# Four changes of order in a two-layer encoder kernel: a copy ahead of maxima, two projection blocks ahead of a value product, final transposes behind a loop, filler products around the opening's sums

## The reference

```python
for l in range(DEPTH):
    mod = cond @ ada_w[l] + ada_b[l]
    sh1, sc1, g1, sh2, sc2, g2 = jnp.split(mod, 6, axis=-1)
    h = modulate(rms_norm(x, norm_mix_g[l]), sh1, sc1)
    if l % 2 == 0:
        y = stick_window_mixer(h, ab_w_in[j], ab_sinks[j], ab_w_out[j])
    else:
        y = hgrn2_mixer(h, hg_w_in[j], lb_all[l], hg_onorm_g[j], hg_w_out[j])
    x = x + g1[:, None, :] * y
    h = modulate(rms_norm(x, norm_ffn_g[l]), sh2, sc2)
    x = x + g2[:, None, :] * conv_ffn(h, ...)
return rms_norm(x, final_g)
```

## Time and profile before

| | |
|---|---|
| median of 3 runs | 1359.72 us |
| lowest, highest | 1358.35, 1359.87 us |
| the profiled execution: its own time | 1360.04 us |
| its span | 1358.2 us, 17432 instructions |
| mean granted clock of TensorE | 0.993 of 2.4 GHz |
| busy: PE, DVE, ACT, POOL | 97%, 60%, 41%, 3% of the span |
| the chain that ended last | PE 89%, DVE 5%, ACT 2% |
| DMA | 160.38 MB, mean 118 GB/s |

### The profile page before, as it was taken

How to read it: one execution, slowest core, us unless ns; L and a number is a source line. 1 busy time by engine, 2 the same in 40 slices (tenths; PEclk the granted TensorE clock), 3 DMA queues, 4 the chain that set the end, 5 groups by cost and what they waited for, 6 DMA issues and landing times.

```text
span 1358.2 us, 17432 instructions
## 1 busy us (share of the span) xinstructions
PE 1323.5 (97%) x6281; PEld 1083.0 (80%) x6281; DVE 808.7 (60%) x1197; ACT 558.1 (41%) x837; POOL 46.9 (3%) x92
## 2 busy tenths in 40 slices
PE   6999998899999999999999999999999999999998
PEld 5877776777888888888778888888788888888786
DVE  5745557567666656436697777775765455552423
ACT  6656554334333333212255555553343333332212
POOL 1000000000000000001100000000000000000000
PEclk9999999999999999999999999999999999999998
DMA  9543431153544555465622222224523333332232
GB/s 336 167 124 109 125 109 32 46 164 103 150 142 143 150 146 147 141 184 190 210 82 78 76 65 63 74 67 125 155 78 95 105 93 93 94 107 93 82 100 81
DMA packets 190148, 160.38 MB, mean 118 GB/s; under 512 B 5271, under 2 KB 163176, under 8 KB 190098
## 3 DMA queue, kind: packets, MB, share of 16 engines
q1 hardware_dynamic: 177696, 116.34, 28.5%
q0 software_dynamic: 11856, 42.68, 10.4%
q10 hardware_dynamic: 546, 0.69, 0.1%
HBM read 157.59 MB, written 2.10 MB: 118 GB/s over the span
## 4 chain that ended last, share of the span: by engine, by line
PE 89%; DVE 5%; ACT 2%; SPq 1%; issue 1%; DMA 1%; DVEq 0%; ACTq 0%
PE proj L1603 61%; PE z L1603 22%; PE obank L1603 3%; PE misc L1603 2%; SPq L479 1%; DVE ada_sum L1118 1%; DMA w_raw<-ab_w_in 1%; DVE normed L1056 0%; ACT w_hi L621 0%; DVE hT_lo L1062 0%; SPq L489 0%; DVE soft L1220 0%; ACT q_sb L741 0%; DVE w_lo L1018 0%; DVE xT L1410 0%
## 5 line engine op out<-in xcount | busy, mean ns | idle before, releaser
L1603 PE MATMUL proj<-hT_hi,w_hi 128*128 128x512 f32 x1112 | 441.5, 397 | 4.6 <-DVE hT_lo L1062 4.1
L1603 PE MATMUL proj<-hT_hi,w_lo 128*128 128x512 f32 x1112 | 433.7, 390 | 0.0
L1603 PE MATMUL proj<-hT_lo,w_hi 128*128 128x512 f32 x1112 | 433.4, 390 | 0.0
L1018 DVE TENSOR_TENSOR w_lo<-w_raw,w_hi 128x1024 fp32r<-128x1024 f32 x189 | 231.2, 1224 | 338.6 <-ACT w_hi L621 338.6
L621 ACT ACTIVATE w_hi<-w_raw 128x1024 fp32r<-128x1024 f32 x191 | 202.0, 1059 | 442.7 <-PE proj L1603 261.2
L1603 PEld LDWEIGHTS proj<-hT_hi,w_hi 128*128 128x128 f32 x1112 | 209.2, 188 | 57.2 <-DVE hT_lo L1062 8.0
L1603 PEld LDWEIGHTS proj<-hT_hi,w_lo 128*128 128x128 f32 x1112 | 209.0, 188 | 44.4
L1603 PEld LDWEIGHTS proj<-hT_lo,w_hi 128*128 128x128 f32 x1112 | 209.3, 188 | 43.3 <-issue 1.7
L1603 PE MATMUL z<-gated_hi,w_hi 128*128 (+1 forms) x264 | 104.5, 396 | 0.2 <-DVE xT L1410 0.2
L1603 PE MATMUL z<-gated_hi,w_lo 128*128 (+1 forms) x264 | 102.8, 389 | 0.0
L1603 PE MATMUL z<-gated_lo,w_hi 128*128 (+1 forms) x264 | 102.8, 389 | 0.0
(11 more groups left out here) (326 smaller groups left out, 1620.6 us busy)
## 6 DMA issues: line engine op xcount, KB each, us to landing
ada_raw<-ada_w POOLq DMA_DIRECT2D x80, 512.0 KB, 4.3
w_raw<-ffn_w_gate SPq DMA_DIRECT2D x44, 512.0 KB, 3.8
w_raw<-ffn_w_up SPq DMA_DIRECT2D x44, 512.0 KB, 3.9
w_raw<-ffn_w_down SPq DMA_DIRECT2D x44, 512.0 KB, 3.4
w_raw<-hg_w_in SPq DMA_DIRECT2D x32, 512.0 KB, 4.1
ada_first<-ada_w SPq DMA_DIRECT2D x16, 512.0 KB, 10.9
w_raw<-ab_w_in SPq DMA_DIRECT2D x14, 512.0 KB, 5.0
w_raw<-ab_w_out SPq DMA_DIRECT2D x8, 512.0 KB, 4.4
```

The lines of the kernel that those rows point to most:

```text
L1018: nc.vector.tensor_tensor(w_lo[:, slot, :], w_raw[:, slot, :], w_hi[:, slot, :].bitcast(F32), ALU.subtract).then_inc(lo_done, 1)
L1603: return nc.tensor.matmul(dst, weights_ap, moving, start=start, stop=stop, skip_group_check=True)
```

## The change

Four places, with nothing computed otherwise but the filler products:

- In the opening, TensorE's wait for the bank misc is moved ahead of its wait for the last sum, with two filler products into misc behind it, and so ahead of first_sums(1). The wait for x_new and the four filler products behind the last x_columns are removed.
- VectorE copies the second bank of window head 0 ahead of the maxima of head 2 and of a split, not behind them.
- In the last round of the window heads, TensorE does blocks 0 and 1 of the first two output units ahead of the values of head 6, not behind them. The two semaphores on which window_values(6) waits first are waited for ahead of these blocks.
- In the last down product, TensorE's sixteen transposes and ScalarE's copy of misc are moved behind the loops over eight units.

```diff
@@ ScalarE, down
                 split(u0 + HALF + 2, 1)
+                with act.Fori(0, HALF // 2 - 1) as i:
+                    for s in range(2):
+                        split(u0 + HALF + 3 + 2 * i + s, s)
                 if last:
                     act.wait_ge(misc_full, MISC_AT["fin"] + 1)
                     nc.scalar.activation(out_nat[:, TB - 1, 0:512], misc[:], ACT.Copy).then_inc(misc_free, 1)
-                with act.Fori(0, HALF // 2 - 1) as i:
-                    for s in range(2):
-                        split(u0 + HALF + 3 + 2 * i + s, s)
@@ VectorE, window heads
             window_norm(1)
+            window_copy(0)
             window_max(2)
             split(U_OUT0 + 1, 1)
-            window_copy(0)
@@ TensorE, opening
             x_columns(range(3, 6))
+            misc_wait("first1")
+            keep_clock(misc, 2)
             pe.wait_ge(first_used, 2 * DC)
-            misc_wait("first1")
             first_sums(1)
             x_columns(range(6, DC))
-            pe.wait_ge(x_new, 6)
-            keep_clock(zb[3], 4)
@@ TensorE, last round of the window heads
                 else:
+                    pe.wait_ge(pt_act, h)
+                    pe.wait_ge(pt_dve, h)
+                    unit_pair(U_OUT0, h_base["o0"], range(0, 2))
                     window_values(h - 1)
-                    unit_pair(U_OUT0, h_base["o0"], range(0, 2))
                     window_transposes(h)
@@ TensorE, down
                 one(u0 + HALF, 1, 0, first=True, mod_group=(8, None)[layer], banks=down_banks[1])
+                with pe.Fori(0, HALF // 2 - 1) as i:
+                    for s in range(2):
+                        one(u0 + HALF + 1 + 2 * i + s, s, 4 * i + 2 * s + 2, banks=down_banks[1])
                 if layer:
                     pe.wait_ge(fin_y, 4)
                     pe.wait_ge(gap_free, len(GAP_MODS))
                     misc_wait("fin")
                     final_transposes(0, range(TB - 1), range(4)).then_inc(fin_full, 1)
                     final_transposes(0, range(TB - 1, TB), range(4)).then_inc(misc_full, 1)
-                with pe.Fori(0, HALF // 2 - 1) as i:
-                    for s in range(2):
-                        one(u0 + HALF + 1 + 2 * i + s, s, 4 * i + 2 * s + 2, banks=down_banks[1])
                 last_two(u0 + FB - 2, 0, FB - 4, down_banks[1])
```

## The result

The changed kernel takes 1353.07 us (median of 5 runs, 1351.51 to 1353.34), the kernel before on the same chip 1359.72 us (5 runs, 1358.35 to 1361.47). The ratio is 0.995, with a 95% interval of 0.9937 to 0.9964: faster by 0.5%, 6.65 us. The profiled execution of the changed kernel took 1352.87 us; its span is 1351.1 us, 7.1 us less than that of before, with a mean granted clock of 0.996. Run again later, beside the last experiments, the same kernel had a median of 1351.7 us (6 runs, 1350.87 to 1353.13) against 1359.96 us, ratio 0.9936 (0.9924 to 0.9948), which is 8.3 us. The two medians of one kernel stand 1.4 us apart, and that difference turned out to be a part of the answer.

A forecast was written before the change was run, and what follows sets the result against it. TensorE, busy 1323.5 of 1358.2 us, was taken as the bound, leaving some 35 us idle plus half-clock stretches. Four gains, 1.0 + 2.4 + 3.4 + 1.6 = 8.4 us, gave 1351.3 us, range 1349.6 to 1354.8.

The forecast's parts named there:

- B: First window heads: VectorE's copy of head 0 ahead of head 2's maxima wins 2.4 us, bounds 0 and 3.3.
- the loop of ScalarE and VectorE takes over: Window heads: exp, norm, max in turn set the pace, so 2.4 us are won, not the 2.63 us wait plus slow clock.
- rival of a loop that gives nothing on: Window heads: slack in the rounds eats the early copy's gain, leaving 0 to -0.65 us; 1353.7 to 1354.3 us, chance 0.12.
- C: Last window heads: two out blocks ahead of head 6's values win 3.4 us, bounds 1.8 and 3.5.
- the clock's part: Out blocks behind the last window heads: without a clock fall, twelve products run at full clock, another 1.6 us won.
- D: Last down product: transposes behind the loop, a 0.45 us wait in place of 2.05, 1.6 us won, bounds 1.2 and 1.9.
- A: Opening: four fillers out, two put ahead of the wait for the sums; second quad group starts earlier, 1.0 us won.
- I take the first: Opening: chosen case that the clock still falls at 42.96 us as now, so the filler edit wins 1.0 us.
- the two fillers keep the clock up: Opening, rival case: no clock fall, second quad group at full clock, 2.0 us won; time 1350.3 us, chance 0.22.
- that likeness: Opening: its transposes and one-column products resemble the mixture before the fall at 1350.24 us, so the clock falls despite two fillers.

The follow-up runs named there:

- the copy in the middle: Changed kernel with VectorE's copy of head 0 between the maxima of head 2 and the split, not ahead of the maxima; 1351.86 us, ratio 0.9944.
- Part A undone: Changed kernel with the opening's two fillers ahead of the sums out and the four behind the x columns back; 1352.1 us, ratio 0.9939.
- part C undone: Changed kernel with the values of head 6 again ahead of out blocks 0 and 1; 1354.31 us, ratio 0.9958.

## Why the prediction was right, and where not

The forecast was 1351.3 us within 1349.6 to 1354.8; 1353.07 and, again, 1351.7 us were measured. The 8.4 us stand against 6.65 and 8.3. Only the second median lies in the forecast's own narrow range (1350.6 to 1352.2). Part by part:

- **B: 2.4 us forecast, 2.52 measured.** The step that mattered, that the loop of ScalarE and VectorE takes over and not TensorE's wait counts, is confirmed by the copy in the middle. The rival of a loop that gives nothing on is out: exp 3 to exp 7 is 22.81 us in every kernel, so what is won ahead of it arrives. What the forecast did not ask is what the old order costs in an execution without the fall at 213.6 us: by the estimate above B is then worth 0.9 us only.
- **C: 3.4 forecast, 3.20 measured.** The wait is shorter by 1.84 us (1.60 for 3.44), as forecast with 1.85, but the stretch by 1.65 only; the clock's part was forecast at 1.58 and is 1.55. Where the other 0.2 us stay was not tried; the new order has one more switch between kinds of product. (The gap left is 3.44 - 1.85 = 1.59 us, measured 1.60, not the 1.65 of the forecast.) The clock's part belongs only to executions with the fall.
- **D: 1.6 forecast, 1.50 measured**; the wait for w_lo is 0.58 instead of 0.45 us. In an execution in which the clock falls behind the old wait it is 3.3, which the bounds (1.2 and 1.9) did not hold.
- **A: 1.0 forecast, 1.46 measured up to exp 0, and for neither of the reasons in the forecast alone.** The step that failed is "I take the first": that the clock falls near 43 us in spite of the two fillers. In none of the ten executions with them did it. I had rested this on the work ahead of the fall at the end of the kernel, as like the opening's; but the same opening fell at 42.93 us in one execution of before and not in the other, so that likeness decides nothing. The other case, "the two fillers keep the clock up", gave 2.0, and that is what is seen where no fall is in the way: from the first quad product to the first score product it took 29.86 us before, with the fall at 42.93, and 27.93 to 27.99 in the five kernels with the two fillers and no fall, 1.9 us less. That the two fillers are what prevents the fall is likely but not shown: of the four executions without them two have it (42.93 and 44.38 us) and two don't. And the prediction had no place for the fall near 27 us. Where it comes, TensorE is late for the sums by itself (in the changed kernel its transposes start at 39.68, 0.66 us later than before), and the two fillers stand on the path and not in idle time. Then the kernel before needs 28.25 us for the same stretch and the one with the fillers 28.52 (both with the fall at 27.14), and part A loses 0.3 us. Part A undone and the changed kernel again, with falls at 27.61 and 27.66, say much the same: 28.46 and 28.69 us. So A is worth between -0.3 and +1.9 us, by the execution. That 1.46 came near the 1.0 of the forecast is luck.
- **The missing term: 1.48 us** for the fall in layer 1. I read the clock's falls of one trace as belonging to the kernel, and so counted those that the change would take away (at full value) and none that another execution would have elsewhere. The second trace of before, with five falls ahead of the end and 1361.88 us, and its first, with three and 1360.04, are the same code.

Compared like with like, the second trace of before against the first of the changed kernel (falls at 27 and at the one-column products in both), the change gains 1360.05 - 1351.07 = 9.0 us of span; of that 1.65 + 1.5 us, and by the estimate above 0.9 us of part B, don't hang on where the falls lie: some 4 us. The other 5 us are falls that the first of these traces has and the second has not, 1.6 us in part B, 1.55 in C and 1.8 in D. Behind B's old wait the clock fell in all three executions that had it, so B's share came in each of them.

The prediction weighed two statements of the Trainium skill, "TensorE: Matmul & The Clock Gate". The one of "What's actually happening", that the point of change differs from run to run since the gate's period is not tied to the kernel's start, agrees with these traces: the same code has its first fall at 42.93 or at 27.14 us. The one of "Why this matters for your kernels", to avoid idle gaps of over about 3 us, does not: the clock fell behind 0.53 us of idleness at 43 us, with no wait of over 0.7 us ahead at 27 us, and behind waits of 2.05 and 2.63 us, but not behind one of 3.44 us in the kernel with part C undone.

## What to carry to other kernels

Before a stretch at half clock is written into a sum, look for it in a second trace of the same kernel: a fall that one execution has and another lacks is worth 1.5 us here and is as large as the edit. Cut both traces at marks around each edit and compare stretch by stretch; differences of 0.1 us can be read that way behind the opening, where the median of five runs moves by 1.4 us. The opening itself scatters more: the first quad product came anywhere from 27.13 to 27.82 us, though the code ahead of it was the same in all but one kernel. Of a wait on the busiest engine, ask which loop of the other engines stands behind it: part B won 2.5 us by removing a wait, and putting 1.5 us of that wait back cost nothing, while the clock stayed up.

## What the runs showed of the hardware that was not expected

In seven executions the clock fell in layer 1 within 2.1 us behind sixteen products of a single column in a row (1.84 us); in the first of the changed kernel TensorE had been busy 2.99 of the 3.40 us before. In four executions with the same row of products it did not fall, nor in the three with these products spread among those of 512 columns. That the row of products is the cause is therefore suggested and not shown. Each fall with TensorE working on lasted 3.4 us at 1.2 GHz and cost 1.5 to 1.7 us. And a short wait that had been harmless in one execution (2.05 us at 1289.96, clock at 1.0) cost 1.6 us more in the next (at 1289.98, fall at 1290.07).
